# Hybrid mixers: half swaps of the rotations by 32-row transfers inside SBUF instead of permutation products

## What is computed

```
def rotary(x, pos):
    half = HEAD_DIM // 2
    inv = jnp.power(ROPE_BASE, -jnp.arange(half, dtype=jnp.float32) / half)
    ang = pos.astype(jnp.float32)[:, None] * inv[None, :]
    cos = jnp.cos(ang)[None, :, None, :].astype(x.dtype)
    sin = jnp.sin(ang)[None, :, None, :].astype(x.dtype)
    x1, x2 = x[..., :half], x[..., half:]
    return jnp.concatenate([x1 * cos - x2 * sin, x1 * sin + x2 * cos], axis=-1)
...
    q = rotary(q.reshape(Bn, S, H, d), pos)
    k = rotary(k.reshape(Bn, S, H, d), pos) * (d ** -0.5)
```

```
    blocks = kv[:, idx] + pos_emb[None, None, :, None, :]
    flat = jnp.moveaxis(blocks, 3, 2).reshape(Bn, nc, G, CMP_BLOCK * d)
    return jax.nn.gelu(flat @ w1) @ w2
```

## Time and profile before

| what | value |
| --- | --- |
| median of 3 runs | 3362.93 us (3362.59 to 3364.24) |
| the profiled execution | 3361.2 us, of which 3359.5 us from its first to its last instruction |
| its mean granted TensorE clock | 0.997 of full speed |
| PE busy | 99% of the span |
| DVE, ACT busy | 59%, 41% |

### The profile page before, as it was taken

How to read it: one execution, slowest core, us unless ns; L and a number is a source line. 1 busy time by engine, 2 the same in 40 slices (tenths; PEclk the granted TensorE clock), 3 DMA queues, 4 the chain that set the end, 5 groups by cost and what they waited for, 6 DMA issues and landing times.

```text
span 3359.5 us, 44342 instructions
## 1 busy us (share of the span) xinstructions
PE 3319.2 (99%) x18719; PEld 2691.5 (80%) x18719; DVE 1983.5 (59%) x2904; ACT 1374.2 (41%) x2102; POOL 31.1 (1%) x68
## 2 busy tenths in 40 slices
PE   8999999999999999999999999999999999999998
PEld 7888878788888888886788888767888887588887
DVE  6554687675546653445564435586765465777644
ACT  4332367443323332326543323365543243654433
POOL 0000003000000000000000000000000000000000
PEclk9999999999999999999999999999999999999999
DMA  5444430244443532231123224211333232023231
GB/s 201 144 144 147 134 122 3 95 135 148 148 147 117 165 107 101 84 100 44 35 91 100 94 99 146 70 38 52 99 101 101 94 144 68 15 82 101 94 100 63
DMA packets 94230, 342.31 MB, mean 102 GB/s; under 512 B 10448, under 2 KB 13008, under 8 KB 93520
## 3 DMA queue, kind: packets, MB, share of 16 engines
q1 hardware_dynamic: 94032, 339.48, 30.6%
HBM read 337.34 MB, written 2.10 MB: 101 GB/s over the span
## 4 chain that ended last, share of the span: by engine, by line
PE 89%; DVE 7%; ACT 3%; issue 1%; DMA 0%; POOL 0%; SPq 0%; ACTq 0%; POOLq 0%; DVEq 0%
PE ps L818 21%; PE ps L819 21%; PE ps L820 21%; PE ps L923 2%; PE ps L924 2%; PE ps L927 2%; PE ps L972 1%; PE ps L974 1%; PE ps L973 1%; DVE SPL L2326 1%; PE ps L948 1%; PE ps L950 1%; PE ps L949 1%; DVE SML L3194 1%; ACT SPH L1613 1%; DVE WK L3210 1%
## 5 line engine op out<-in xcount | busy, mean ns | idle before, releaser
L2326 DVE TENSOR_TENSOR SPL<-RAW,SPH 128x1024 fp32r<-128x1024 f32 x522 | 635.9, 1224 | 871.0 <-ACT SPH L1613 870.6
L1613 ACT ACTIVATE SPH<-RAW 128x1024 fp32r<-128x1024 f32 x522 | 548.2, 1056 | 971.9 <-PE ps L820 869.3
L818 PE MATMUL ps<-HH,SPH 128*128 128x512 f32 x2312 | 910.0, 394 | 1.6 <-DVE SPL L2326 1.2
L820 PE MATMUL ps<-HH,SPL 128*128 128x512 f32 x2312 | 900.1, 389 | 0.0
L819 PE MATMUL ps<-HL,SPH 128*128 128x512 f32 x2312 | 900.0, 389 | 0.0
L818 PEld LDWEIGHTS ps<-HH,SPH 128*128 128x128 f32 x2312 | 434.0, 188 | 103.1 <-issue 10.8
L819 PEld LDWEIGHTS ps<-HL,SPH 128*128 128x128 f32 x2312 | 434.1, 188 | 92.1 <-issue 3.6
L820 PEld LDWEIGHTS ps<-HH,SPL 128*128 128x128 f32 x2312 | 434.0, 188 | 90.7
L818 PE MATMUL ps<-AH,SPH 128*128 128x512 f32 x996 | 389.0, 391 | 0.7 <-DVE AH L2678 0.7
L820 PE MATMUL ps<-AH,SPL 128*128 128x512 f32 x996 | 387.6, 389 | 0.0
L819 PE MATMUL ps<-AL,SPH 128*128 128x512 f32 x924 | 359.5, 389 | 0.0
(11 more groups left out here) (571 smaller groups left out, 4311.6 us busy)
## 6 DMA issues: line engine op xcount, KB each, us to landing
RAW<-in_ws SPq DMA_DIRECT2D x522, 512.0 KB, 3.3
RAW<-in_wa SPq DMA_DIRECT2D x96, 512.0 KB, 3.5
WK<-in_sm SPq DMA_DIRECT2D x2, 2784.0 KB, 10.2
WK<-in_cst SPq DMA_DIRECT2D x2, 1664.0 KB, 7.4
X<-in_x SPq DMA_DIRECT2D x8, 256.0 KB, 8.0
out<-X SPq DMA_DIRECT2D x16, 128.0 KB, 1.8
WK<-in_sm SPq DMA_DIRECT2D x1, 768.0 KB, 4.9
PCT<-in_pc SPq DMA_DIRECT2D x1, 349.0 KB, 2.8
```

The source lines that it names most:

```text
L818: e.matmul(out, wh, rhs[0], start=start, stop=False)
L820: mm = e.matmul(out, wl, rhs[0], start=False, stop=stop)
L1613: e.activation(SPH[:, q:q + 1024], RAW[:, r:r + 1024], ACT.Copy).then_inc(hi_ready.did(("hi", n)))
L2326: e.tensor_tensor(SPL[:, q:q + 1024], RAW[:, r:r + 1024], SPH[:, q:q + 1024].bitcast(F32), ALU.subtract).then_inc(lo_ready.did(("lo", n)))
```

## The change

The product is taken away. ACT, at the place of the rotation in its own program, starts four transfers, each of 32 partitions x 512 (64 KB), from the tile to the scratch tile, with the 32-row halves exchanged. They count up a semaphore of their own for each of the four tiles. DVE waits for all four before it multiplies the scratch tile by SIN in place; the signs, which the permutation carried, are now in the SIN table. PE has no part in the rotation, and the bank ring has four uses fewer in each hybrid mixer.

```diff
-    c["sin"] = np.tile(np.sin(ang.astype(np.float64)), (4, 1))
+    c["sin"] = np.tile(np.sin(ang.astype(np.float64)), (4, 1)) * np.where(np.arange(128) % 64 < 32, -1.0, 1.0)[:, None]
...
+        rot_landed = {u: signal(f"s_rotated{u}_landed") for u in (2, 3, 4, 5)}
...
                     if what == "rot":
-                        ps.plan(("rot", s, x[0]), ("rsin", s, x[0]))
                         scr.plan(("rq", s, x[0]), ("rope", s, x[0]))
...
-                        if what == "rot":
-                            u = x[0]
-                            w.wait_ge(("pj", s, u), ("tables1", s), *ps.before("rot", s, u))
-                            e.matmul(ps["rot", s, u][:], H["PERM"], wk(u), start=True, stop=True).then_inc(
-                                pe_done.did(("rot", s, u)))
-                        elif what == "compress":
+                        if what == "compress":
...
-                        if what == "compress":
+                        if what == "rot":
+                            u = x[0]
+                            w.wait_ge(("pj", s, u), *scr.before("rq", s, u))
+                            for p0 in range(0, 128, 32):
+                                p1 = p0 + 32 if p0 % 64 == 0 else p0 - 32
+                                e.dma_start(scr["rq", s, u][p0:p0 + 32, :], wk(u)[p1:p1 + 32, :]).then_inc(
+                                    landing(rot_landed[u], ("rot", s, u)), 16)
+                        elif what == "compress":
...
-                            w.wait_ge(("rot", s, u), *scr.before("rq", s, u))
-                            e.tensor_tensor(q, ps["rot", s, u][:], H["SIN"], ALU.mult).then_inc(
-                                dve_done.did(("rsin", s, u)))
+                            w.wait_ge(("rot", s, u), ("tables1", s))
+                            e.tensor_tensor(q, q, H["SIN"], ALU.mult).then_inc(dve_done.did(("rsin", s, u)))
                             e.tensor_tensor(wk(u), wk(u), H["COS"], ALU.mult).then_inc(dve_done.did(("rcos", s, u)))
-                            w.wait_ge(("rcos", s, u))
+                            w.wait_ge(("rcos", s, u), ("rsin", s, u))
                             e.tensor_tensor(wk(u), wk(u), q, ALU.add).then_inc(dve_done.did(("rope", s, u)))
```

## The result

The changed kernel takes 3378.39 us at the median of its runs (3374.6 to 3394.7), the kernel before 3362.76 (3357.1 to 3365.8). The medians differ by 15.6 us; the ratio of the runs is 1.0055, 95% interval 1.0047 to 1.0064, which is 18.5 us. The forecast's sum was 8.9 us. The direction and the mechanism came out as forecast; the size is 1.8 to 2.1 times the forecast's.

The account below looks back on a forecast made before the run. PE, busy 99% of the span, was taken as the bound. Removed products (-6.9 us), new waits (+10.4) and clock (+5.4) gave +8.9 on the profiled 3361.2; with the median 1.7 above it, 3372 us was forecast, range 3362 to 3381.

Parts of the forecast that it names:

- The forecast's sum: Over both hybrid mixers: -6.9 us of products, +10.4 of PE waits, +5.4 of clock, so +8.9 us.
- The direction: Whole kernel: slower, 3372 us forecast, +0.27%; slower by over 0.2% was given a chance of 0.52.
- the mechanism: At "compress v" in each mixer, PE waits 5.2 us for DVE's Gv, late behind the transfers, and its clock falls.

Follow-up runs that it names:

- experiments 1 to 3 and 5: The changed kernel with, in turn, transfers issued early (3369.73 us), no transfer (3368.98), Gv ahead of two rotations on DVE (3368.68), one 128-row transfer per rotation (3375.56).

## What to carry to other kernels

Work taken off the busiest engine is worth the slack of whoever feeds it next; look for that slack first, and for idle time of the feeder where its work can be moved, since the change cost 16 us with the transfers where they stood in the queue and gained 6 us with the same transfers, and DVE's work on them, where two engines had been idle. A wait on TensorE can have a second price, the clock after it: here 3.0 to 3.5 us up to the retention products in the changed kernel. Of the eight waits of 2.8 to 6.1 us in experiments 1 to 3 and 5, six cost 2.7 to 3.1 us in this way, one 1.6 and one nothing. Transfers issued by a compute engine take its time one by one (0.6 us here for 64 KB and for 256 KB), so do not count on a margin of a few tenths to hide two groups of eight in front of something urgent.

## What the runs showed of the hardware

A transfer of 64 KB within SBUF issued on ACT took its queue 0.61 us at the median, with the next 0.64 us behind, and landed 2.1 us after its start at the median, 3.9 at most in the changed kernel; one of 256 KB took the queue 0.56 us and landed after 4.8. SP's issue beside it took 0.33 us. A wait of TensorE of 2.75 to 2.77 us was followed by half the clock in three of four cases, one of 2.13 us was not; and filling both mixers' waits with products nobody reads gained 8.2 us. A fall of the clock at "compress v" was followed by a second one some 70 us later in ten mixers of ten.
